# Token tiles begun one by one in front of the RWKV inputs and the queries of a two-block layer kernel

## The reference

```python
mem_n = rms_norm(mem, mem_norm_g)
h = rms_norm(x, g[0])
p = h @ w_in_first                                  # 2816 columns
y_conv = conformer_conv(p[..., :2 * D_CONV], ...)   # value * sigmoid(gate), 31 taps, layer norm, silu
y_rwkv = rwkv7_mix(p[..., 2 * D_CONV:], ...)
x = x + rms_norm(concatenate([y_conv, y_rwkv]) @ w_out, g[1])
# queries of rms_norm(x, g[2]) against keys and values mem_n @ wkv
x = x + rms_norm(memory_cross_attention(rms_norm(x, g[2]), mem_n, wq, wkv, wo), g[3])
x = x + rms_norm(swiglu(rms_norm(x, g[4]), w_gu, w_down), g[5])
```

## Time and profile before

| | us |
|---|---|
| median of 3 runs | 880.26 |
| lowest, highest | 880.02, 882.04 |
| profiled execution, its time | 882.02 |
| profiled execution, its span | 880.1 |
| PE busy | 849.9 (97%) |
| DVE busy | 566.1 (64%) |
| ACT busy | 444.4 (50%) |

### The profile page before, as it was taken

One profiled execution on the slowest core, in us unless ns is written; L12 is line 12 of the kernel. 1 busy time (PEld: TensorE's weight loads), 2 busy tenths in 40 slices (PEclk: granted clock), 3 DMA queues, 4 the chain that ended last, 5 costly groups with the idle time before them and its releaser, 6 DMA issues.

```text
span 880.1 us, 18506 instructions
## 1 busy us (share of the span) xinstructions
PE 849.9 (97%) x7964; PEld 790.2 (90%) x7964; DVE 566.1 (64%) x667; ACT 444.4 (50%) x568; POOL 20.9 (2%) x31
## 2 busy tenths in 40 slices
PE   4999999999999999999999999999999999999997
PEld 4899999998999998888998888888887999999885
DVE  5386564576887777637799885567654655545443
ACT  5465757354755655636474511446555544443432
POOL 1110000000000002000000000000000000000000
PEclk9999999999999999999999999999999999999999
DMA  8754444565655555555552301235524455555551
GB/s 311 252 197 141 147 144 147 189 215 182 247 187 191 189 172 179 175 191 177 183 175 100 134 7 51 98 125 198 181 96 144 167 191 185 170 175 186 191 191 48
DMA packets 22256, 145.92 MB, mean 166 GB/s; under 512 B 2618, under 2 KB 2810, under 8 KB 6064
## 3 DMA queue, kind: packets, MB, share of 16 engines
q1 hardware_dynamic: 19008, 134.23, 44.1%
q0 software_dynamic: 2896, 10.13, 3.3%
q10 hardware_dynamic: 288, 0.59, 0.2%
HBM read 143.87 MB, written 1.07 MB: 165 GB/s over the span
## 4 chain that ended last, share of the span: by engine, by line
PE 85%; DVE 5%; DMA 4%; ACT 4%; issue 1%; POOL 0%; DVEq 0%; ACTq 0%; SPq 0%
PE ps L1688 24%; PE ps L1690 23%; PE ps L1689 23%; PE ps L1811 3%; PE ps L2160 2%; DMA bias<-bias_scratch 2%; PE ps L2123 1%; ACT w_hi L477 1%; DMA raw<-in_weights 1%; PE ps L1754 1%; DMA norm_gain<-in_rows_vec 1%; PE ps L1729 1%; DVE w_lo L981 1%; PE ps L2356 1%; PE ps L2372 1%
## 5 line engine op out<-in xcount | busy, mean ns | idle before, releaser
L981 DVE TENSOR_TENSOR w_lo<-raw,w_hi 128x2048 fp32r<-128x2048 f32 x125 | 287.3, 2301 | 137.4 <-ACT w_hi L477 137.3
L1688 PE MATMUL ps<-hT_hi,w_hi 128*128 128x256 f32 x1144 | 326.2, 285 | 1.0 <-ACT sig L631 0.9
L1689 PE MATMUL ps<-hT_lo,w_hi 128*128 128x256 f32 x1144 | 323.6, 283 | 0.0
L1690 PE MATMUL ps<-hT_hi,w_lo 128*128 128x256 f32 x1144 | 323.6, 283 | 0.0
L477 ACT ACTIVATE w_hi<-raw 128x2048 fp32r<-128x2048 f32 x125 | 238.8, 1913 | 146.9 <-DMA raw<-in_weights 146.8
L1688 PEld LDWEIGHTS ps<-hT_hi,w_hi 128*128 128x128 f32 x1144 | 219.4, 192 | 5.4 <-issue 3.0
L1689 PEld LDWEIGHTS ps<-hT_lo,w_hi 128*128 128x128 f32 x1144 | 219.5, 192 | 0.1
L1690 PEld LDWEIGHTS ps<-hT_hi,w_lo 128*128 128x128 f32 x1144 | 219.4, 192 | 0.0
L1690 PE MATMUL ps<-w_hi,gT_lo 128*128 128x512 f32 x176 | 69.3, 394 | 0.0
L1689 PE MATMUL ps<-w_lo,gT_hi 128*128 128x512 f32 x176 | 68.8, 391 | 0.0
L1688 PE MATMUL ps<-w_hi,gT_hi 128*128 128x512 f32 x176 | 68.7, 390 | 0.0
(11 more groups left out here) (305 smaller groups left out, 1132.4 us busy)
## 6 DMA issues: line engine op xcount, KB each, us to landing
raw<-in_weights SPq DMA_DIRECT2D x126, 1024.0 KB, 4.9
row_gain<-in_rows_vec POOLq DMA_DIRECT2D x4, 512.0 KB, 4.2
norm_gain<-in_rows_vec POOLq DMA_DIRECT2D x4, 512.0 KB, 5.2
bias<-bias_scratch POOLq DMA_DIRECT2D x1, 1536.0 KB, 11.0
x<-in_x SPq DMA_DIRECT2D x2, 512.0 KB, 4.8
xn<-in_mem POOLq DMA_DIRECT2D x2, 512.0 KB, 5.9
out<-x SPq DMA_DIRECT2D x4, 256.0 KB, 2.0
masks<-in_masks POOLq DMA_DIRECT2D x1, 768.0 KB, 10.6
```

The lines of the kernel that those rows point to most:

```text
L981: V.tensor_tensor(w_lo[:, n % RAW, :], raw[:, n % RAW, :], w_hi[:, n % RAW, :].bitcast(F32), ALU.subtract).then_inc(sems["lo_ready"], 1)
L1688: mm(dst, left[0], right[0], start=first, stop=False)
L1689: mm(dst, left[0], right[1], start=False, stop=False)
L1690: return mm(dst, left[1], right[0], start=False, stop=last)
```

## The change

Stages and counts:

```diff
-MEM_A, MEM_B, MEM_C = 2, 5, 1
+MEM_A, MEM_B, MEM_C = 1, 5, 2
-STAT_ORDER[14:18] = [("y3", 0), ("g4", 0), ("y3", 1), ("g4", 1)]
+for _at, _names in ((6, ("ln_f", "g0")), (10, ("y1", "g2")), (14, ("y3", "g4"))):
+    STAT_ORDER[_at:_at + 2 * TT] = [(_name, _t) for _t in range(TT) for _name in _names]
```

```diff
-            sumsq("ln_f", lambda t: x[:, t, :], x_tile("down"), lambda: splits(n_a + 1))
-            sumsq("g0", lambda t: x[:, t, :], x_tile("ln_f"))
-            for i in range(MEM_A - 1):
-                memory_out(i)
-                splits(n_a + i + 2)
-            fill_normed("g0")
-            memory_out(MEM_A - 1)
+            sumsq_tile("ln_f", "down", 0)
+            sumsq_tile("g0", "ln_f", 0)
+            sumsq_tile("ln_f", "down", 1)
+            splits(FIRST_SLAB["in2"])
+            fill_tile("g0", 0)
+            sumsq_tile("g0", "ln_f", 1)
+            memory_out(0)
+            fill_tile("g0", 1)
             splits(FIRST_SLAB["in2"] + 1)
...
             for i in range(11):
+                if i == 2:
+                    act.wait_ge(sems["first_turned"], 3)
+                    A(glu[:, 2:4, TAPS - 1:], bank(7).rearrange("p (a n) -> p a n", a=2), ACT.Copy)\
+                        .then_inc(sems["glu_out"], 1)
...
             splits(FIRST_SLAB["mem_c"])
             root_table(1)
-            sumsq("y1", lambda t: banks(4 + 2 * t, 2), acc_tile("out2"))
-            sumsq("g2", lambda t: x[:, t, :], x_tile("y1"))
+            sumsq_acc("y1", "out2", 0)
+            sumsq_tile("g2", "y1", 0)
+            sumsq_acc("y1", "out2", 1)
+            fill_tile("g2", 0)
+            sumsq_tile("g2", "y1", 1)
             splits(FIRST_SLAB["wq"])
+            memory_out(6)
+            fill_tile("g2", 1)
             memory_out(7)
-            fill_normed("g2")
```

DVE:

```diff
-            splits(n_a)
-            add_acc("down")
+            splits(n_a - 1)
             dve.wait_ge(sems["row_gain_in"], 16)
...
-            normed("g0")
-            fill_normed("g0")
+            add_acc("down", (0,))
+            splits(n_a)
+            final_norm(0)
+            add_acc("down", (1,))
+            normed("g0", (0,), 2)
+            final_norm(1)
+            fill_tile("g0", 0)
             splits(FIRST_SLAB["in2"])
+            normed("g0", (1,), 2)
+            fill_tile("g0", 1)
...
-            TAPS_FIRST = {2: 2, 3: 2, 4: 3, 5: 3, 6: 2, 7: 2, 8: 2}
-            TAPS_AFTER = {1: 2, 7: 5, 8: 5}
+            TAPS_FIRST = {3: 2, 4: 3, 5: 3, 6: 2, 7: 2, 8: 2}
+            TAPS_AFTER = {7: 5, 8: 5}
...
                 splits(min(n0 + i + 2, FIRST_SLAB["mem_b"] - 1))
+                if i == 2:
+                    dve.wait_ge(sems["glu_out"], 1)
+                    conv_taps(4)
                 if i in IN2["value"]:
...
+                    dst = gate if i == 1 else glu[:, 2 * half:2 * half + 2, TAPS - 1:]
...
             splits(FIRST_SLAB["mem_c"])
-            add_normed("y1", 1)
-            normed("g2")
-            fill_normed("g2")
+            add_normed("y1", 1, tiles=(0,))
+            normed("g2", (0,), 2)
+            add_normed("y1", 1, lambda: fill_tile("g2", 0), tiles=(1,))
+            normed("g2", (1,), 2)
+            fill_tile("g2", 1)
             splits(FIRST_SLAB["wq"])
```

```diff
+            def turn_in2():
+                u = FIRST_UNIT["in2"] + 1
+                pe.wait_ge(out_freed[u % 2], u // 2 + 1)
+                turn_first(rwide("tmp")[:, 512:1024], bank(7))
...
-                        if name and i == last - 1 and j == 7:
-                            transposes(name, 0)
-                            transposes(name, 1)
+                        if i == last - 1 and j in places:
+                            transposes(name, places.index(j))
-            memory_slabs(0, MEM_A, "g0")
+            memory_slabs(0, MEM_A, "g0", (8,))
...
-            for i in range(11):
-                if i == 0:
-                    operand(FILL["g0"], KD - 1)
+            first_pair("in2", "g0")
+            for i in range(2, 11):
...
-                    used(features(n0 + i, u0 + i, None))
+                    used(features(n0 + i, u0 + i, None, between=turn_in2 if i == 2 else None))
...
-            token_products("out2", hT, out_ready)
-            memory_slabs(7, 8, None)
+            token_products("out2", hT, out_ready, together=2)
+            memory_slabs(8 - MEM_C, 8, "g2", (3, 10))
```

More of the change, by code:

```diff
@@ L104 @@
 X_READY = {"w_o": 0, "down": 2, "ln_f": 4, "y1": 6, "y3": 8, "y5": 10}
+X_AT = {"w_o": (1, 2), "down": (3, 5), "ln_f": (4, 6), "y1": (7, 8), "y3": (9, 10)}
 LEVELS = 6
@@ L709, in memory_out, with sumsq_tile, fill_tile @@
                 evacuated(u, A(dst, src, ACT.Copy))
-            root_table(0)
-            sumsq("ln_f", lambda t: x[:, t, :], x_tile("down"), lambda: splits(n_a + 1))
-            sumsq("g0", lambda t: x[:, t, :], x_tile("ln_f"))
-            for i in range(MEM_A - 1):
-                memory_out(i)
-                splits(n_a + i + 2)
-            fill_normed("g0")
-            memory_out(MEM_A - 1)
+            def sumsq_tile(name, after, t):
+                sumsq(name, lambda t: x[:, t, :], x_tile(after), tiles=(t,))
+            def fill_tile(name, t):
+                for half in range(2):
+                    fill_part(name, t, half)
+            sumsq_tile("ln_f", "down", 0)
[6 more added lines that the diff above has]
+            fill_tile("g0", 1)
             splits(FIRST_SLAB["in2"] + 1)
@@ L920, in _ @@
             root_table(0)
[L922 to L928, removed]
-            splits(FIRST_SLAB["gu2"])
[L930 to L936, removed]
+            sumsq_acc("y3", "wo2", 0)
+            splits(FIRST_SLAB["gu2"])
+            sumsq_tile("g4", "y3", 0)
+            sumsq_acc("y3", "wo2", 1)
+            fill_tile("g4", 0)
+            sumsq_tile("g4", "y3", 1)
+            fill_tile("g4", 1)
             def gu_pair(p, turn=0):
@@ L1312, in _, with final_norm, fill_tile @@
             fill_memory()
-            splits(n_a)
-            add_acc("down")
+            splits(n_a - 1)
             dve.wait_ge(sems["row_gain_in"], 16)
-            for t in range(TT):
-                if t:
-                    splits(n_a + 1)
+            def final_norm(t):
                 V.scalar_tensor_tensor(out=x[:, t, :], in0=x[:, t, :], scalar=inverse_rms("ln_f", t),
                                        in1=row_gain[:, :], op0=ALU.mult, op1=ALU.mult).then_inc(sems["x_ready"], 1)
-            normed("g0")
-            fill_normed("g0")
+            def fill_tile(name, t):
+                for half in range(2):
+                    fill_part(name, t, half, 2 * t + half)
+            add_acc("down", (0,))
[5 more added lines that the diff above has]
+            fill_tile("g0", 0)
             splits(FIRST_SLAB["in2"])
+            normed("g0", (1,), 2)
+            fill_tile("g0", 1)
             do(V.memset(glu[:, :, 0:TAPS - 1], 0.0))
@@ L1633, in _ @@
             normed("g4", (0,), 2)
[L1635 to L1639, removed]
+            add_normed("y3", 2, lambda: fill_tile("g4", 0), tiles=(1,))
             normed("g4", (1,), 2)
-            for half in range(2):
-                fill_part("g4", 1, half, 2 + half)
+            fill_tile("g4", 1)
             def gu_pair(p, turn=0):
@@ L2020, in feed_loop @@
                 n0, u0 = FIRST_SLAB[name], FIRST_UNIT[name]
+                transposes(norm, 0)
                 first_pair(name, norm, (lambda: turn_up(0)) if name == "up" else None)
@@ L2060, in _, with memory_slabs @@
             operand(FILL["mem"], KD - 1)
-            def memory_slabs(first, last, name):
+            def memory_slabs(first, last, name, places):
                 for i in range(first, last):
                     for j, _ in enumerate(memory_slab(i)):
-                        if name and i == last - 1 and j == 7:
-                            transposes(name, 0)
-                            transposes(name, 1)
-            memory_slabs(0, MEM_A, "g0")
+                        if i == last - 1 and j in places:
+                            transposes(name, places.index(j))
+            memory_slabs(0, MEM_A, "g0", (8,))
             def loras():
```

21 lines of the change are left out of this document (12 added, 9 removed).

## The result

The changed kernel takes 891.68 us (median of 4 runs, 890.25 to 892.05), the kernel before 880.28 us beside it (4 runs, 880.02 to 882.04): a ratio of 1.0121 [1.0108, 1.0134], slower by 1.2%. The profiled execution took 891.93 us, with a span of 890.1 us; the one of before took 882.02, with 880.1.

What follows compares the result with a forecast made beforehand. PE was taken as the bound, busy 849.9 of 880.1 us. Terms -2.3 + 0.45 + 4.4 + 5.4 + 4.0 = +12.0 us on the profiled 882.02 gave 894.0, set to 892.2 us against the median; range 884.5 to 895.3.

Steps and rivals of the forecast that it cites:

- The old stops of in2, -2.3 us: PE's two stops at transposes in front of in2 (1.35 and 0.54 us) vanish: -2.3 us.
- 0.45: In in2, the four added transposes of `turn_in2` cost PE +0.45 us.
- The stop at the turning, +4.4: At `turn_in2`, PE waits for slab 1's gate-by-value product, behind the split and load of slab 4: +4.4 us.
- The queries late, +5.4 and +2.0 for the clock: First queries slab waits for wq 0's late split: +5.4 us, stop of 3.1 us inside; half clock +2.0.
- The clock, +2.0 per place: Half clock behind the long stops: +2.0 us at the turning and +2.0 at wq 0, bounds 0 and 2.5 each.
- The shift of slab 2, "hidden by 1 us": In in2, DVE's shift of slab 2 ends at 436.4, PE wants the bank at 437.5: hidden by 1 us.
- the turning does not wait: Rival at `turn_in2`: the gate-by-value product is earlier than the load chain says; 885.8 us, chance 0.08.
- The middle, 0: From the low-rank products to the memory slab ahead of the queries: the forecast sum has no term there.
- The rival "faster": Tile-by-tile norms close both old stops, at in2 and the queries, the price only the turning: 875.9 us, chance 0.06.

Runs made afterwards that it cites:

- e7_both: Changed kernel with the edits of `e5_taps_split` and `e6_queries` together: 875.91 us, ratio 0.9942 to the kernel before.
- e5_taps_split: `e1_product_first` with two of four convolution taps and the shift of in2 slab 2 ahead of the split of slab 5: 885.29 us.
- e2_wq_split_early: Changed kernel, but ACT and DVE split queries slab 0 ahead of the operand of tile 0 of g2: 886.56 us.
- e4_y1_ahead: Changed kernel, but DVE finishes y1 of tile 1 before the low part of g2 tile 0: 890.12 us.
- e6_queries: Changed kernel with queries slab 0 split early, y1 tile 1 finished first and g2 tile 0 transposed one memory slab earlier: 881.86 us.
- medians of the pair: `e8_queries_busy` and its twin `e9_queries_again`, 11 runs of each on one chip: 880.48 and 882.13 us.
- e3_busy_stop: Changed kernel with 36 matmuls whose result nobody reads ahead of the wait at the turning: 889.63 us.
- e1_product_first: Changed kernel, but for in2 slab 1 DVE multiplies gate by value before it splits slab 4: 890.11 us.
- e8_queries_busy: `e6_queries` with 36 matmuls whose result is overwritten in the stop at the turning: 880.48 us, ratio 0.9996 to the kernel before.
- e9_queries_again: `e6_queries` once more, unchanged, as the twin of `e8_queries_busy` on the same chip: 882.13 us, ratio 1.0013 to the kernel before.

## Why the prediction was right, step by step

- **The old stops of in2, -2.3 us.** Both gone. No trace has this term alone. `e7_both` has it with the turning: -1.95, forecast -2.3 + 0.45 = -1.85.
- **The stop at the turning, +4.4.** 4.25 us, released by the link that was named. Everything lies 1.4 us earlier than forecast, because the program reached the first memory slab so much earlier. The chain from "slab 0 used" (the last 24 of the pair's matmuls start at 414.90) to the end of the product (424.33 + 0.68) is 10.1 us, forecast 10.2. `e5_taps_split` confirms that it is an order and no shortage of engine time.
- **The queries late, +5.4 and +2.0 for the clock.** +6.9 against 7.4. The first stop 3.12 (3.1), the second 2.65 (3 to 4). The queries start 20.87 us behind the memory slab; the forecast was 630.7 - 609.8 = 20.9. `e2_wq_split_early` and `e4_y1_ahead` show the two causes apart, and `e6_queries` that with both gone, and tile 0 turned earlier, nothing of the loss stays.
- **The clock, +2.0 per place.** The sign was right, and 2.0 lies within what was found, but it is not one number. At the turning 1.65 us is left of it in the medians of the pair. In the profile of the changed kernel, where the clock was down for about 7 us, it is more: 43.60 - 36.51 - 4.25 = 2.8 us. At the queries no run measured it alone; from the first queries product to the first scores the changed kernel took 13.10 us (628.15 to 641.25) and `e6_queries`, at full clock, 11.51 (619.10 to 630.61), which makes about 1.6.
- **What the clock term rested on.** The sentence that the prediction quotes from the Trainium skill (TensorE: Matmul & The Clock Gate, What's actually happening), "the default state is throttled, and activity releases the throttle", agrees with the pair: PE busy with work that nobody reads stayed at 1.00. The prediction's step from there, that each long stop costs a stretch at half clock and that the stop of 1.55 us bears this out, was too firm. A stop of 1.54 or 1.55 us was followed by half clock in seven traces and not in four. The prediction read its price, 2.0 us, from the rows right behind it: 5.95 us to the matmul at 688.02. `e6_queries`, at full clock, took 4.44 us for the same rows (681.43 to 685.87), so the price was 1.5 us there, and in the whole last stretch 0.7. The stop of 3.1 us in front of tile 1 of `g2` was followed by 0.50 in the changed kernel, `e2_wq_split_early` and `e3_busy_stop`, but by 1.00 in `e1_product_first` and `e5_taps_split`, where the clock fell only in the next stop. Of the stops in the middle of the program, those of 4.09 to 4.45 us had it down in every trace that has one.
- **The shift of slab 2, "hidden by 1 us".** True of the changed kernel, where PE wanted the bank late because it had stood at the turning and then run slowly. But the cover was the stop and the 2.0 us of clock themselves: with the clock up PE waited 0.43 us for this shift (`e8_queries_busy`), with the stop gone too 3.15 us (`e1_product_first`). I worked out this margin and didn't carry it over to the kernel in which the stop is gone, and so forecast 885.4 for `e1_product_first`. The same error is in the forecast of the rival "the turning does not wait", 885.8: with the product early enough, 890.1 was measured.
- **The middle, 0.** It came out -0.6 in the changed kernel, and the stretch is between 164.4 and 165.3 us in the others. The cause is not known.

The sum: +5.1 (forecast 4.55), +6.9 (7.4), -0.6 (0) is +11.4, beside +12.0 forecast and 11.4 between the medians. The errors of the terms are of either sign, so part of the closeness is luck. The sum leaves out the start of the program (-1.4): the profiled execution of before was the slowest of its four, and whether the medians share the difference can't be seen, since only profiled executions have a trace.

The rival "faster" was put at 875.9 us, on the condition that the product of slab 1 is done at the turning and wq 0 split ahead of tile 1. The code doesn't meet it. `e7_both` does, with more orders changed than the rival had, and took 875.91 us. Its two terms came out as well: -1.95 where it had -1.85 (the old stops less the turning), and -2.49 where it had -2.5. That the total agrees to 0.01 us is luck all the same: the profile has another -0.55 and -0.8 us in stretches that the rival put at nothing.

Left open: the stop of 1.55 us at the second feed-forward, which is in the trace of before and of after alike; no kernel was run against it.

## What to carry to other kernels

For every wait that a change adds, go to the engine that releases it and read what stands ahead of the releasing instruction in its order: here 0.68 us of product stood behind a 2.29 us split, behind a load. A stop is also a cover: before a fix is priced, recompute each slack downstream with the stop gone, since 4.25 us removed at the turning, and the clock with it, gave back 1.6 us (891.68 to 890.11; 2.4 us in the stretch of the traces) until the next late reader was moved as well. The length of a stop is no measure of what holds PE when the work ahead of it ran at another clock: compare starts along the chain. Where work ahead is counted in slabs ("one slab past the first memory slab"), putting one more slab into the sequence silently shifts what is prepared early; here it put a queries slab's weights behind its own operand.

## What the hardware showed that I had not expected

36 more matmuls made a kernel 1.65 us faster (882.13 to 880.48 us). Their second stretches differ by 1.7 us (43.34 and 41.62), and what differs in them is the granted clock. And the stretch with the stop at the turning differed by up to 1.4 us between kernels with the same code in it: 43.60 in the changed kernel and 43.34 in `e9_queries_again`, but 42.17 in `e2_wq_split_early`, 42.35 in `e6_queries` and 42.69 in `e4_y1_ahead`, whereas the two kernels without any stop there had 36.51 and 36.51. The traces show what was different: the clock was at 0.50 for about 7 us in the first two and for about 3.5 us in the other three, each time from the last microsecond or so of a stop of 4.17 to 4.45 us on. These windows of `e2_wq_split_early` stand beside the last two of the twin above (0.50 and 0.82):

```profile
428.00:430.00 2.00, 2.00 (x18) 2.00 (x17) 0.94 (x1) 0.96 (x1) 0.00 (x0) 0.93 0.00 0
430.00:432.00 2.00, 2.00 (x19) 2.00 (x19) 2.00 (x3) 0.84 (x2) 0.00 (x0) 1.00 0.30 49
```

What decides, in one execution or another, whether the clock falls behind a stop and for how long, no run here shows. A comparison of a few us that has such a stop in it needs more than four runs.
